# A hybrid decoder layer: memory rows, mixer input and mixed rows turned by VectorE and small DMAs in place of eleven runs of TensorE transposes

## The reference

```
h = x + 1/2 * post1(SwiGLU_1(pre1(x)))          # w_gu 2048 x 11264, w_down 5632 x 2048
u = pre_mix(h);  P = u @ W_in                   # columns shared out among the head groups
y_gla, y_gdn, y_xa = three mixers of P (gated linear attention, gated delta
                     rule, cross-attention to 256 memory tokens), each @ w_up
mk, mv = split(rmsnorm(mem, mem_norm) @ w_mem_kv)
m = (sig(g1)*y_gla + sig(g2)*y_gdn + sig(g3)*y_xa) @ W_out
h = h + post_mix(m)
h = h + 1/2 * post2(SwiGLU_2(pre2(h)))
```

## Time and profile before

| | us |
|---|---|
| median of 3 runs | 2524.53 (2524.22 to 2524.65) |
| the profiled execution | 2523.52 |
| its span, first to last instruction | 2521.9 |
| granted TensorE clock, mean | 0.999 of full |
| PE busy | 2504.0 (99%) |
| DVE busy | 1392.4 (55%) |
| ACT busy | 1233.9 (49%) |

### The profile page before, as it was taken

One profiled execution on the slowest core, in us unless ns is written; L12 is line 12 of the kernel. 1 busy time (PEld: TensorE's weight loads), 2 busy tenths in 40 slices (PEclk: granted clock), 3 DMA queues, 4 the chain that ended last, 5 costly groups with the idle time before them and its releaser, 6 DMA issues.

```text
span 2521.9 us, 33217 instructions
## 1 busy us (share of the span) xinstructions
PE 2504.0 (99%) x11467; PEld 2075.3 (82%) x11467; DVE 1392.4 (55%) x1555; ACT 1233.9 (49%) x1510; POOL 278.5 (11%) x512
## 2 busy tenths in 40 slices
PE   8999999999999999999999999999999999999998
PEld 7888888888888888888888888888888888888887
DVE  5555555554455456676675564465655555555444
ACT  6444444454445456757575544444644444443443
POOL 4212121200011001101010000000111121211000
PEclk9999999999999999999999999999999999999999
DMA  7777777766678655555554666666677676767664
GB/s 246 209 201 210 202 209 202 202 205 193 193 218 260 194 174 142 158 141 150 141 153 140 192 191 193 194 239 191 208 208 205 200 212 202 208 200 251 194 189 158
DMA packets 297384, 490.48 MB, mean 194 GB/s; under 512 B 23116, under 2 KB 96976, under 8 KB 296528
## 3 DMA queue, kind: packets, MB, share of 16 engines
q1 hardware_dynamic: 279712, 455.16, 60.7%
q0 software_dynamic: 16464, 32.06, 4.0%
q10 hardware_dynamic: 1120, 2.10, 0.2%
HBM read 469.30 MB, written 8.39 MB: 189 GB/s over the span
## 4 chain that ended last, share of the span: by engine, by line
PE 98%; ACT 1%; DVE 1%; DMA 0%; issue 0%; SPq 0%; DVEq 0%; POOLq 0%; ACTq 0%; POOL 0%
PE acc L545 91%; PE acc L587 1%; PE acc L570 1%; PE mix L605 1%; PE mix L853 1%; DMA raw<-w_ffn_gu 0%; PE mix L830 0%; PE mix L820 0%; PE mix L777 0%; PE mix L810 0%; ACT whi L989 0%; PE mix L711 0%; PE mix L822 0%; PE mix L746 0%; DVE nat L1504 0%
## 5 line engine op out<-in xcount | busy, mean ns | idle before, releaser
L1444 DVE TENSOR_TENSOR wlo<-raw,whi 128x1024 fp32r<-128x1024 f32 x860 | 1053.9, 1229 | 909.1 <-ACT whi L989 905.7
L989 ACT ACTIVATE whi<-raw 128x1024 fp32r<-128x1024 f32 x860 | 910.1, 1060 | 1192.7 <-PE acc L545 1166.4
L545 PE MATMUL acc<-whi,x_hi 128*128 128x512 f32 x1616 | 629.6, 390 | 0.0
L545 PE MATMUL acc<-whi,x_lo 128*128 128x512 f32 x1616 | 628.8, 389 | 0.0
L545 PE MATMUL acc<-wlo,x_hi 128*128 128x512 f32 x1616 | 628.6, 389 | 0.0
L545 PE MATMUL acc<-whi,u_hi 128*128 128x512 f32 x896 | 360.1, 402 | 0.0
L545 PEld LDWEIGHTS acc<-whi,x_lo 128*128 128x128 f32 x1616 | 303.3, 188 | 63.2
L545 PEld LDWEIGHTS acc<-wlo,x_hi 128*128 128x128 f32 x1616 | 303.3, 188 | 62.7
L545 PEld LDWEIGHTS acc<-whi,x_hi 128*128 128x128 f32 x1616 | 303.3, 188 | 62.6
L545 PE MATMUL acc<-whi,u_lo 128*128 128x512 f32 x896 | 349.6, 390 | 0.0
L545 PE MATMUL acc<-wlo,u_hi 128*128 128x512 f32 x896 | 349.4, 390 | 0.0
(11 more groups left out here) (339 smaller groups left out, 1572.4 us busy)
## 6 DMA issues: line engine op xcount, KB each, us to landing
raw<-w_ffn_gu SPq DMA_DIRECT2D x352, 512.0 KB
raw<-w_ffn_down SPq DMA_DIRECT2D x176, 512.0 KB
raw<-w_in SPq DMA_DIRECT2D x224, 256.0 KB
raw<-w_in SPq DMA_DIRECT2D x96, 512.0 KB
raw<-w_mem_kv SPq DMA_DIRECT2D x32, 512.0 KB
raw<-w_out SPq DMA_DIRECT2D x32, 512.0 KB
nat<-nat POOLq DMA_DIRECT2D x352, 32.0 KB, 3.6
raw<-w_in SPq DMA_DIRECT2D x64, 128.0 KB
```

The lines of the kernel that those rows point to most:

```text
L545: ins = nc.tensor.matmul(acc[:, par, t, :], x[:, k0 + k, cols], w[:, s, k, :], start=first and k == 0 and m == 0, stop=last and k == UK - ...
L989: act(whi[:, s], raw[:, s], ACT.Copy).then_inc(hi_ready, 1)
L1444: tt(wlo[:, s], raw[:, s], whi[:, s].bitcast(fp32), ALU.subtract).then_inc(lo_ready, 1)
```

## The change

The memory rows (four blocks of 512 columns), the mixer input (four) and three of the four mixed pieces are turned in the second way. TensorE's eleven runs of eight transposes are gone; the fourth mixed piece keeps its run, and so do x and h. In their place:

- VectorE turns a block (`turn_rows`, two instructions of 128x512), GpSimd swaps its squares (`swap_rows`, sixteen DMAs), and, some slots later, ScalarE scales (`upper_turned`, four instructions of 128x256, or one of 128x1024 for a mixed piece) and VectorE takes the low part (`lower_turned`, eight instructions of 128x128).
- Memory rows: turned in slots 10, 17, 24, 31 of down1 and scaled six slots later. Mixer input: turned in slots 4, 8, 12, 16 of the memory projection and scaled seven slots later (11, 15, 19, 23). Mixed pieces: turned in slot 12 of up0, 0 of gates1, 12 of up1 and scaled seven slots later.
- New buffers: `u_turn` (two, each turned and swapped), `m_turned`, `m_swapped`. The memory rows use the buffers of the activations.
- TensorE waits for `rows_lo` at the start of the memory projection, of the first head group and of out.
- The squares for the norm of h move to slots 4, 8, 12, 16, and its sum from slot 11 to slot 17. Those of the first block of down1's product move to slot 40.

```diff
@@ -63,12 +63,16 @@
 
 
 
+MEM_AT, MEM_TIME = (10, 17, 24, 31), 6
+U_AT, U_TIME = (4, 8, 12, 16), 7
+M_TIME = 7
+R_MEMORY, R_MIXIN, R_MIXED = 0, 4, 8
 STEP_AT = ([0, 1, None, 2, 3, 4, 5, None] + list(range(6, 26)) + [None, 26, None] + 32 * [None])
 
 TAKE_AT = [U_D - 1, 2 * U_D - 1, STEP_AT.index(22) + 2, 4 * U_D - 1, 5 * U_D - 1, 6 * U_D - 1]
 
 
-T_X, T_MEM, T_U, T_M, T_H2 = 0, 4, 8, 12, 16
+T_X, T_M3, T_H2 = 0, 4, 5
 
 R_X, R_MEM, R_D1, R_H1, R_OUT, R_H2, R_D2 = range(7)
...
+        def swap_quarters(dst, src, done):
+
             for j in range(4):
                 for q in range(4):
-                    pl.dma_start(swapped[32 * j:32 * j + 32, q * 256:(q + 1) * 256],
-                                 turned[32 * q:32 * q + 32, j * 256:(j + 1) * 256]).then_inc(sem("act_swapped"), 16)
+                    nc.gpsimd.dma_start(dst[32 * j:32 * j + 32, q * 256:(q + 1) * 256],
+                                        src[32 * q:32 * q + 32, j * 256:(j + 1) * 256]).then_inc(done, 16)
...
+            def swap_rows(r, dst, src, before):
+
+                pl.wait_ge(sem("rows_turned"), r + 1)
+                if before:
+                    pl.wait_ge(sem("rows_lo"), before)
+                swap_quarters(dst, src, rows_swapped(r)[0])
+
+            def swap_u(c):
+
+                swap_rows(R_MIXIN + c, u_turn[:, c % 2, 1, :], u_turn[:, c % 2, 0, :], R_MIXIN + c - 1 if c >= 2 else 0)
...
             pl.engine_nop().then_inc(sem("act_lo"), 1)
             for c in range(4):
                 if c == 2:
                     for n in range(N_GU):
-                        swap_quarters(n)
+                        swap_act(n)
+                    pl.wait_ge(sem("act_lo"), N_GU + 1)
                 if c >= 2:
-                    pl.wait_ge(t_done, T_MEM + c - 1)
+                    swap_rows(R_MEMORY + c - 2, swapped, turned, c - 2)
                     pl.wait_ge(sem("squared"), 8 * R_MEM + 2 * (c - 1))
                 pl.dma_start(res[:, c % 2], mem_v[:, :, c * CW:(c + 1) * CW]).then_inc(sem(f"mem_in{c % 2}"), 16)
+            swap_rows(R_MEMORY + 2, swapped, turned, 2)
+            swap_rows(R_MEMORY + 3, swapped, turned, 3)
             rsqrt(R_MEM)
 
-            pl.wait_ge(t_done, T_MEM + 4)
             fetch(0)
             fetch(1)
             rsqrt(R_D1, True)
             for c in range(4):
+                if c == 2:
+                    swap_u(0)
                 store_h(0, c)
                 if c + 2 < 4:
                     fetch(c + 2)
+            for c in range(1, 4):
+                swap_u(c)
             rsqrt(R_H1)
 
             pl.wait_ge(unit_used, UB["mem"])
...
+            swap_rows(R_MIXED, m_swapped, m_turned, 0)
+            swap_rows(R_MIXED + 1, m_swapped, m_turned, R_MIXED + 1)
             pl.wait_ge(unit_used, UB["up1"])
             fetch_block(1, a["n_mix_post"])
+            swap_rows(R_MIXED + 2, m_swapped, m_turned, R_MIXED + 2)
             rsqrt(R_OUT, t=0)
             rsqrt(R_OUT, t=1)
             for c in range(4):
...
 
                 def between(j):
-                    if f == 0 and i == 0 and j in (3, 8, 13, 18):
-                        c = (j - 3) // 5
-                        pe.wait_ge(sem(f"mem_in{c % 2}"), 16 * (c // 2 + 1))
-                        transposed(T_MEM + c, res[:, c % 2], c % 2)
                     if i == 0 and j == U_F - 3:
 
                         pe.wait_ge(sem("act_lo"), (f + 1) * N_GU + 1)
...
                     j += 2 * U_D * i
-                    if j in (3, 5, 7, 9):
-                        c = (j - 3) // 2
-                        pe.wait_ge(sem("h_ready"), c + 1)
-                        transposed(T_U + c, nat[:, :, c * CW:(c + 1) * CW], c % 2, min(c, 1))
                     if j in (12, 25):
...
 
+                pe.wait_ge(sem("rows_lo"), R_MEMORY + 4)
                 for i in range(2):
                     for half in range(2):
...
-            def mixture(n):
-
-                pe.wait_ge(sem("m_ready"), n + 1)
-                transposed(T_M + n, msum[:, :, :], 0)
+                          (lambda j: mixer_steps(j, mixed)) if mixed is not None else None)
 
             def up(p):
 
...
+
+                for k in range(4):
+                    ins = act(by_token(dst)[:, k], by_block(src)[:, k], ACT.Copy, scale=vecT[:, gain + k:gain + k + 1])
+                ins.then_inc(done, 1)
 
             def take_out(n, par, dst, k):
 
...
@@ -1132,14 +1175,14 @@
 
             def memory():
                 def tasks(j):
-                    if j in (3, 5, 7, 9):
-                        c = (j - 3) // 2
-
-                        ac.wait_ge(unit_used, UB["mem"])
-                        upper(T_U + c, u_hi[:, 4 * c:4 * c + 4, :], c % 2, KT_D + 4 * c)
-                    if j in (4, 6, 8, 10):
-                        c = (j - 4) // 2
+                    if j in U_AT:
+                        c = U_AT.index(j)
+                        ac.wait_ge(sem("h_ready"), c + 1)
                         squares(R_H1, c, nat[:, :, c * CW:(c + 1) * CW])
+                    if j - U_TIME in U_AT:
+                        c = U_AT.index(j - U_TIME)
+                        ac.wait_ge(*rows_swapped(R_MIXIN + c))
+                        upper_turned(u_hi[:, 4 * c:4 * c + 4, :], u_turn[:, c % 2, 1, :], KT_D + 4 * c, sem("rows_hi"))
...
             def mixture(n):
-                upper(T_M + n, x_hi[:, 4 * n:4 * n + 4, :], 0, scale=0.5)
+
+                ac.wait_ge(*rows_swapped(R_MIXED + n))
+                act(blocks(x_hi[:, 4 * n:4 * n + 4, :]), m_swapped.rearrange("p (q b l) -> p b q l", q=4, l=32), ACT.Copy,
+                    scale=0.5).then_inc(sem("rows_hi"), 1)
 
             def up(p):
...
 
+            def turn_rows(dst, src, done):
+
+                for t in range(NT):
+                    ins = nc.vector.transpose(dst.rearrange("p (j k t l) -> p t k j l", j=4, t=NT, l=32)[:, t],
+                                              src[:, t, :].rearrange("p (k j l) -> p k j l", j=4, l=32))
+                ins.then_inc(done, 1)
+
+            def lower_turned(dst, hi, src, gain, done):
+
+                for k in range(4):
+                    for t in range(NT):
+                        scale = 0.5 if gain is None else vecT[:, gain + k:gain + k + 1]
+                        ins = stt(by_token(dst)[:, k, t], by_block(src)[:, k, t], scale, by_token(hi)[:, k, t].bitcast(fp32),
+                                  ALU.mult, ALU.subtract)
+                ins.then_inc(done, 1)
+
             def take_product(n, par, b, c):
...
                         residual(0, R_D1, (j - 1) // 2)
-                    if j in (3, 5, 7, 9):
-                        c = (j - 3) // 2
+                    if j in U_AT:
+                        c = U_AT.index(j)
+                        ve.wait_ge(unit_used, UB["mem"])
+                        ve.wait_ge(sem("h_ready"), c + 1)
+                        turn_rows(u_turn[:, c % 2, 0, :], nat[:, :, c * CW:(c + 1) * CW], sem("rows_turned"))
+                    if j - U_TIME in U_AT:
+                        c = U_AT.index(j - U_TIME)
                         rows = slice(4 * c, 4 * c + 4)
-                        lower(T_U + c, u_lo[:, rows, :], u_hi[:, rows, :], c % 2, KT_D + 4 * c)
-                    if j == 11:
+                        ve.wait_ge(sem("rows_hi"), R_MIXIN + c + 1)
+                        lower_turned(u_lo[:, rows, :], u_hi[:, rows, :], u_turn[:, c % 2, 1, :], KT_D + 4 * c, sem("rows_lo"))
...
 
             def mixture(n):
+
+                ve.wait_ge(sem("rows_hi"), R_MIXED + n + 1)
                 rows = slice(4 * n, 4 * n + 4)
-                lower(T_M + n, x_lo[:, rows, :], x_hi[:, rows, :], 0, scale=0.5)
+                lower_turned(x_lo[:, rows, :], x_hi[:, rows, :], m_swapped, None, sem("rows_lo"))
 
             def up(p):
```

More of the change, by code:

```diff
@@ L137, in hybrid_layer @@
              ("wsml", [P, KT_D, 32], f32r), ("small_T", [32, SEQ], fp32)],
+            [("below_turn", [P, 60, SEQ], fp32), ("u_turn", [P, 2, 2, NT * CW], fp32)],
             [("below_post", [P, 80, SEQ], fp32), ("post_a", [P, 2, CW], fp32)],
@@ L918, in gate_logits @@
                     chunk(at(UB[f"gates{p}"], 0, 0, k * U_D), k * U_D, U_D, u_hi, u_lo, k % 2, QB[f"gates{p}"] // 2 + k // 2,
-                          (lambda j: mixer_steps(j, mixed)) if mixed is not None else
-                          (lambda j: mixture(2 * p - 1) if j == 1 else None))
-            def mixture(n):
-                pe.wait_ge(sem("m_ready"), n + 1)
-                transposed(T_M + n, msum[:, :, :], 0)
+                          (lambda j: mixer_steps(j, mixed)) if mixed is not None else None)
             def up(p):
@@ L933, in up @@
                         chunk(UB[f"up{p}"] + k * U_O, k * U_O, U_O, o_hi[:, br], o_lo[:, br], k % 2,
[L934 removed]
+                              QB[f"up{p}"] // 2 + k // 2)
             def output():
@@ L1111, in tasks @@
                         upper_act((f + 1) * N_GU - 1, act_hi[:, KT_F - 4:KT_F, :])
```

(35 more changed lines are left out.)

52 lines of the change are left out of this document (34 added, 18 removed).

## The result

| | us |
|---|---|
| changed kernel, median | 2528.02 (2525.06 to 2530.81, 20 runs) |
| kernel before, beside it | 2524.13 (2523.1 to 2525.92, 20 runs) |
| ratio | 1.0015, 95% interval 1.0009 to 1.0022 |
| span of the profiled execution | 2527.2 (before 2521.9) |
| granted TensorE clock, mean | 0.998 |

The changed kernel is slower by 0.15%, 3.9 us. I had predicted 2522.9 and a range up to 2528. The profiled execution is 5.3 longer than the one of before, so all that follows explains 5.3 and not 3.9.

The account below looks back on a forecast made before the run. TensorE, busy for 99% of the span, was taken to set the time. The terms -10.0 + 7.2 + 1.2 gave -1.6 us: 2521.9 on the profiled execution, 2522.9 as the predicted median, range 2517 to 2528.

Parts of the forecast that it names:

- TensorE's loss of work: Eleven runs of transposes leave TensorE: 3.48 us memory rows, 3.9 mixer input, 2.61 mixed rows, 10.0 in all.
- come 1.9 us early: In all eleven groups, VectorE's split low half of a weight is ready 1.9 us before TensorE wants it.
- I cost these at nothing: Waits for swapped rows, in memory rows, mixer input and mixed rows, were put at 0 us.
- The 1.5 us to spare: Memory rows in down1: the swap's DMAs land 1.5 us before the copies that want the rows.
- Slots 3 to 9: Memory projection: weights already late there hold TensorE up around units 9 to 12, 1.2 us, between 0 and 3.5.
- The second rival: Starved weight loads in slots 3 to 16 of the memory projection: 11 us in place of 1.2, 2532.7; chance 0.07.
- Its remark that the departing lowers make room: Argument against starved loads: low parts leave these slots of the memory projection, so weight loads are asked for sooner.
- Slot 20: Memory projection: small weights, loaded late behind GpSimd's swaps, make TensorE wait 7.2 us at unit 24, between 5.3 and 10.7.
- The port rule: Rival: GpSimd's DMA issues slow beside VectorE, 8 us more in the swap of block 3, 2531; chance 0.03.
- Eight short operations: VectorE's low part per group, eight multiply-subtracts of 128x128, takes 2.26 us, bounds 1.22 and 2.7; page estimate 1.55.
- What was to show it: Signs expected in the trace: transposes gone from TensorE, waits at unit 24 and for `wsm`, small waits around units 9 to 12.
- TensorE waiting once: Sign: TensorE waits once, 5 to 10 us, at unit 24 of the memory projection for the low half of the weights.

Follow-up runs that it names:

- e1: Kernel before with only the three mixed pieces turned by VectorE and DMAs: 2521.56 us against 2524.22, ratio 0.9991.
- e11: Changed kernel with the mixer input turned by TensorE as before and memory rows turned in slots 10, 18, 26, 34 of down1: 2517.58 us, ratio 0.9973.
- e4: Changed kernel with the split of the small weights in slot 28 in place of 20: 2521.47 us, ratio 0.999.
- e5: Changed kernel with the two loads of the small weights ahead of the swap of block 2 in GpSimd's queue: 2521.78 us, ratio 0.999.
- e6: Changed kernel with memory rows turned in slots 10, 18, 26, 34 of down1 in place of 10, 17, 24, 31: 2525.53 us, ratio 1.0005.
- e3: Kernel before with only the four blocks of the mixer input turned by VectorE and DMAs: 2531.1 us, ratio 1.0027.
- e7: Changed kernel with the mixer input scaled nine slots after its turn in place of seven: 2529.87 us, ratio 1.0023.

## Why the prediction failed

- **TensorE's loss of work, -10.0.** Right. The mixed pieces alone give -2.7 for 2.6 (e1), and with the memory rows well placed seven runs give -6.4 for 6.1 (e11).
- **The failed step: low halves that "come 1.9 us early, a pattern that all eleven groups share", and the waits of which it says "I cost these at nothing".** The working had the raw weights there on time and the swap landing after 3.6 us. For the mixed pieces it held. In down1 it did not: 2.9 us of waits, 3.5 with all of the two stops and the slower matmuls behind them. The 1.5 us to spare rested on the median landing of 352 DMAs, where the last of sixteen was wanted, and that landed after 6.5 to 7.0. The same rows had a maximum of 5.2, and that alone would have left nothing. The late raw weights took another 1.2. In the mixer input the swapped rows were in time, but the raw unit 15 was 5 us late with the low part of block 0 behind it: 2.19 of waiting, 4.1 with its stop and half clock. Together some 7.6 us stood where the sum has 0, and that turns -1.6 into a loss.
- **Slots 3 to 9, 1.2 "between 0 and 3.5".** What I had looked at, units 9 to 12, cost 0.74 and 0.32 of waits, 1.7 with the stops and the slower matmuls: the size was right. That the same late loads would meet a new task at unit 15 I had not seen. The second rival, starved loads with 11 us at most and a chance of 0.07, named late loads; with unit 15 about half of its price was paid. Its remark that the departing lowers make room had left out that they come back in slots 11 to 23.
- **Slot 20, 7.2.** The place, the chain and the signs were as predicted. It cost 4.47 + 0.16 + 1.7 = 6.4 (6.5 and 6.2 by e4 and e5). The wait itself was 2.7 shorter: the landing was 3.1 shorter (4.5 for 7.6), the links ahead of it 0.4 longer. The half clock, for which the sum had no term here or at unit 15, gave 1.7 of it back.
- **The port rule.** The swaps took 7.82 to 7.87, 496 to 597 ns each over 528 issues, beside a VectorE at 0.56. The Trainium skill (SBUF — State Buffer, section "SBUF: two separate sides") has such DMAs locked out by VectorE's two-port work; no run here shows it for them, and none shows that VectorE's operations here are of that kind.
- **Eight short operations.** Taken at 2.26, measured 2.19. The Trainium skill (VectorE: DVE Perf Modes, section "The TRN2 errata") led to an estimate of 1.55; the measurement decides. The same section says that this row under-predicts the duration of a single operation.
- **What was to show it.** ScalarE's wait for `wsm`, the wait at unit 24 (4.47, a little under the 5 to 10) and small waits at units 9 and 11 came. "TensorE waiting once" and "no wait of ScalarE for swapped rows" didn't hold.

By the terms, each with its stops and slower matmuls: slot 20 at 6.4 for 7.2 is -0.8, slots 3 to 9 at 1.7 for 1.2 is +0.5, unit 15 +4.1 and down1 +3.5 for nothing, the start and the head groups -0.1, and the eleven runs gave 0.3 more than the 10.0. That is 6.9 over the -1.6 of the sum, and so the 5.3 of the spans.

## What to carry to other kernels

Taking work off the engine that sets the time brings new tasks to its feeders. Before crediting it, look in each stretch at how late the feeders can be there: a slack that is worked out with every load on time is no slack where loads are late already. Take the landing of a batch of DMAs from the last of it and not from the median, with the traffic that it will run beside. A queue that is worked in order carries every delay to what stands behind it, so a load with a fixed use is issued ahead of steps that wait for something late. Where the parts of a change have different cover, keep those that pay: here seven of eleven runs moved give 6.4 us, all eleven lose 3.9 as first placed, and 4.8 to 4.9 us are gained with all eleven placed better.

## What the hardware did that I had not expected

- After a stop of TensorE of 2.19 us or more (nine stops away from the start of the kernel, up to 7.44) the granted clock fell to half, 1.2 for 2.4 GHz, for some seven to thirteen matmuls. That cost 1.7 to 1.8 us more in seven cases, 2.6 in e6 (behind 5.36) and 2.9 in e3 (behind 4.93). After stops of 0.3 to 1.60 it didn't fall, nor after one of 2.10 (e4). A late weight therefore costs more than its lateness once it is late enough.
- The load of `wsm` landed in 4.5 to 5.0 us here and in 7.5 to 7.7 before. In the four kernels where TensorE came to stand for it (after, e3, e6, e7) it took 3.8 to 5.9, in the others 5.9 to 8.3. The DMA engines' share was 0.91 and 0.92 in the stretches of after and before, but the weights' own queue had 0.31 of them in after (806 to 812 us) and 0.61 before (779 to 788). That would fit a load that lands sooner because ScalarE and VectorE stand too and few weights are asked for; no run shows it by itself.
- In the reciprocal root of two columns on GpSimd the second operation took 0.71 us as a rule, and once 4.11 (e4); the first, 1.2 or less, once took 4.22 (e5). Both stood within a microsecond behind a swap's issues. I can't say what makes it.
